# The low halves of the weights in one or in two VectorE instructions: a hybrid encoder with product-key experts, on one core

## The reference, cut to what matters

```
def peer(h, w_query, sub_keys, expert_down, expert_up):
    q = (x @ w_query).reshape(T, PEER_HEADS, 2, D_HALF)
    s = jnp.einsum('thcd,hckd->thck', q, sub_keys).astype(jnp.float32)
    ...
    top_s, pos = lax.top_k(cand, PEER_TOPK)
    idx = jnp.take_along_axis(cidx, pos, axis=-1)
    gate = jax.nn.softmax(top_s, axis=-1).astype(h.dtype)
    ...
        a = jax.nn.gelu(jnp.einsum('cd,chkd->chk', xc, expert_down[ic]))
        return jnp.einsum('chk,chkd->cd', a * gc, expert_up[ic])
```

## Time and profile before

| | us |
|---|---|
| median of three runs | 2186.85 (2167.92 to 2192.66) |
| the profiled execution | 2204.12 |
| its span, first to last instruction | 2202.2 |
| PE busy in it | 1969.0 |
| DVE busy | 1379.8 |
| POOL busy | 666.6 |
| mean granted TensorE clock | 0.933 of full speed |

### The profile page before, as it was taken

How to read it: one execution, slowest core, us unless ns; L and a number is a source line. 1 busy time by engine, 2 the same in 40 slices (tenths; PEclk the granted TensorE clock), 3 DMA queues, 4 the chain that set the end, 5 groups by cost and what they waited for, 6 DMA issues and landing times.

```text
span 2202.2 us, 38709 instructions
## 1 busy us (share of the span) xinstructions
PE 1969.0 (89%) x12144; PEld 1772.9 (81%) x12144; DVE 1379.8 (63%) x2960; ACT 1003.9 (46%) x1638; POOL 666.6 (30%) x627
## 2 busy tenths in 40 slices
PE   7977779668889999999999988797778889999998
PEld 6776779668879888888889987696778788888887
DVE  6855557557535776676567766474556535677666
ACT  5632436245435455444444434353435335544553
POOL 1314538747720000000102023666657710000000
PEclk9988879879989999999999998898889989999999
DMA  6943435334436878888659733353344446787775
GB/s 216 382 159 96 134 114 170 117 107 151 144 127 206 253 243 246 290 287 282 232 168 321 253 134 116 114 173 106 117 127 136 153 134 222 243 241 242 242 241 190
DMA packets 159299, 419.97 MB, mean 191 GB/s; under 512 B 32396, under 2 KB 66220, under 8 KB 158733
## 3 DMA queue, kind: packets, MB, share of 16 engines
q1 hardware_dynamic: 130268, 369.23, 52.5%
q0 software_dynamic: 28976, 50.17, 6.7%
HBM read 382.30 MB, written 37.00 MB: 190 GB/s over the span
## 4 chain that ended last, share of the span: by engine, by line
PE 81%; issue 7%; another core or an unknown queue 5%; ACT 4%; DVE 3%; DMA 1%; POOL 0%; SPq 0%; DVEq 0%; ACTq 0%; POOLq 0%
PE psum L1246 26%; PE psum L1248 26%; PE psum L1247 26%; ACT w_hi L457 1%; DVE w_lo L705 1%; ACT L604 1%; PE psum L1435 1%; ACT L646 1%; PE psum L1412 1%; PE psum L1328 0%; PE psum L1339 0%; ACT big L636 0%; PE psum L1365 0%; DMA raw<-in_attn_units 0%
## 5 line engine op out<-in xcount | busy, mean ns | idle before, releaser
L705 DVE TENSOR_TENSOR w_lo<-raw,w_hi 128x1024 fp32r<-128x1024 f32 x636 | 772.6, 1219 | 455.1 <-ACT w_hi L457 346.0
L1246 PE MATMUL psum<-x_hi,w_hi 128*128 128x256 f32 x2576 | 767.0, 298 | 131.8 <-issue 66.1
L457 ACT CAST w_hi<-raw 128x1024 fp32r<-128x1024 f32 x636 | 663.2, 1048 | 347.1 <-PE psum L1248 330.4
L1247 PE MATMUL psum<-x_lo,w_hi 128*128 128x256 f32 x2576 | 756.7, 294 | 30.0 <-issue 29.5
L1248 PE MATMUL psum<-x_hi,w_lo 128*128 128x256 f32 x2576 | 755.1, 293 | 30.9 <-issue 30.4
L393 POOL DMA_INDIRECT gates<-whole,address x512 | 592.3, 1157 | 408.3 <-issue 159.7
L1246 PEld LDWEIGHTS psum<-x_hi,w_hi 128*128 128x128 f32 x2576 | 519.6, 202 | 160.4 <-issue 101.6
L1248 PEld LDWEIGHTS psum<-x_hi,w_lo 128*128 128x128 f32 x2576 | 519.5, 202 | 35.8 <-issue 35.6
L1247 PEld LDWEIGHTS psum<-x_lo,w_hi 128*128 128x128 f32 x2576 | 520.5, 202 | 33.3 <-issue 32.1
L1246 PE MATMUL psum<-w_hi,l_hi 128*128 128x512 f32 x1152 | 451.5, 392 | 3.4 <-DVE l_lo L1185 2.2
L1248 PE MATMUL psum<-w_hi,l_lo 128*128 128x512 f32 x1152 | 448.5, 389 | 0.0
(11 more groups left out here) (143 smaller groups left out, 1133.6 us busy)
## 6 DMA issues: line engine op xcount, KB each, us to landing
raw<-in_down SPq DMA_DIRECT2D x256, 512.0 KB
raw<-in_up SPq DMA_DIRECT2D x256, 512.0 KB
raw<-in_sg_units SPq DMA_DIRECT2D x72, 512.0 KB
gates<-zeros POOLq DMA_DIRECT2D x64, 512.0 KB, 7.5
g_t<-gates SPq DMA_DIRECT2D x248, 128.0 KB, 4.4
raw<-in_query SPq DMA_DIRECT2D x32, 512.0 KB
raw<-in_attn_units SPq DMA_DIRECT2D x20, 512.0 KB
gates<-whole,address POOLq DMA_INDIRECT x512
```

Source lines behind the costliest of these rows:

```text
L457: act.copy(w_hi[n % SPLIT][:, :], raw[n % RAW][:, :]).then_inc(hi_done, 1)
L705: dve.tensor_tensor(w_lo[n % SPLIT][:, :], raw[n % RAW][:, :], w_hi[n % SPLIT][:, :].bitcast(F32), ALU.subtract).then_inc(lo_done, 1)
L1246: pe.matmul(out_ap, hi_s, hi_m, start=start, stop=False)
L1247: pe.matmul(out_ap, hi_s, lo_m, start=False, stop=False)
```

## The change

In the query and the down stage DVE makes the subtraction of a unit in two instructions of 512 columns, one directly behind the other. The wait for `hi_done` stands ahead of the first, and the increment of `lo_done` is on the second. All other stages keep the single instruction of 1024 columns.

```diff
+            def split_lo_halves(n):
+
+                dve.wait_ge(hi_done, n + 1)
+                for b in range(2):
+                    c = slice(D // 2 * b, D // 2 * b + D // 2)
+                    ins = dve.tensor_tensor(w_lo[n % SPLIT][:, c], raw[n % RAW][:, c], w_hi[n % SPLIT][:, c].bitcast(F32),
+                                            ALU.subtract)
+                ins.then_inc(lo_done, 1)
+
...
                 for c in range(QUERY_UNITS):
-                    split_lo(u["query"] + c + AHEAD)
+                    split_lo_halves(u["query"] + c + AHEAD)
                     dve.wait_ge(s_done, QUERY_UNITS * layer + c + 1)
...
                 def low(n):

-                    split_lo(u["down"] + n + AHEAD)
+                    split_lo_halves(u["down"] + n + AHEAD)
```

## The result

The changed kernel takes 2247.8 us (median of four runs, 2234.83 to 2262.30), the kernel before, run beside it, 2189.76 us (2167.92 to 2213.56). The ratio is 1.030 with a 95% interval of 1.019 to 1.041: slower by 3%, where 2.2% was forecast. The ratio leaves out before's run of 2213.56 us, which counts as a slow one, so it is larger than that of the two medians, which lie 58 us apart. The profiled execution of after took 2244.87 us, 40.8 us more than that of before.

The account below looks back on a forecast made before the run. PE, starved in the query and down stages by the pace of POOL's scatter, bounds the kernel. 45 us lost on PE plus 2 us of DVE on 2204.1 us give 2251, at the median 2235 us; range 2165 to 2305 us.

Parts of the forecast that it names:

- the likeliest case: Whole program: the forecast itself, 2235 us, in a band of 2210 to 2265 us; chance 0.42.
- What bounds the kernel: Query and down stages: PE is starved more the faster POOL issues the scatter; some 295 us lost in the two.
- DVE's own time: Subtraction in query and down: two halves take 0.08 us more, 23 us over 288 units, 2 us counted.
- POOL's locks: Indirect DMAs held by DVE's two-input instructions: halves let POOL in sooner, locks of 101 us fall 21%.
- always-through: POOL always gets through between the halves: locks 52% less, L393's mean 1055 ns, 2299 us; chance above 2265 us 0.14.
- The slope: Query and down: PE loses 2.1 us for each us by which a DMA comes sooner, 45 us in all.
- The signs: Changed profile: L393's mean about 1115 ns, "issue" and eviction waits grow, mean clock below 0.933, up stages and mixers unchanged.
- Never-through: POOL never gets between the halves: locks 9% more, 2170 us; chance 0.23 together with no cause.
- DVE alone: DVE's 23 us are not hidden and POOL changes nothing: 2210 us; chance 0.05.
- Only a companion: The scatter's rate only accompanies PE's stalls: 2170 to 2190 us; chance 0.23 together with never through.
- Faster: POOL never through, longer locks lift windows to a spacing of 1.6 us and more: 2152 us; chance 0.16.
- the prediction's two sentences: Trainium skill: two-input DVE instructions contend with GpSimd reading SBUF; against it, a probe where tensor_tensor did not stall such DMAs.

Follow-up runs that it names:

- the pauses: Three small POOL memsets behind each indirect DMA of the kernel before: 2063.27 us, 0.931 of before's median; with the halves 2046.77 us, 0.924.
- the 64-value DMAs: The kernel before with each indirect DMA writing the values of 64 partitions in place of 128: 2375.99 us, 1.072 of before's median.
- quarters: The subtraction of a query or down unit in four instructions of 256 columns: 2335.03 us, 1.059 of before.

## Why the prediction was right

The time came 13 us above the forecast 2235, inside the 2210 to 2265 of the likeliest case. Step by step:

**What bounds the kernel.** 295 us lost in the two stages were read off the windows; taking the scatter away gave back 292, of which the stages of the profiles account for 272. That the rate is the cause, and not the scatter's presence alone, was argued then and is shown by the pauses (slower pace, 7% faster) and the 64-value DMAs (faster pace, 7% slower).

**DVE's own time.** The forecast was 0.61 us from half to half, 23 us of DVE, 2 us on the path. A half takes 688 ns, the pair 0.07 us more than the single instruction (1.29 us, and not 1.38), DVE is 22 us busier, and without the scatter the halves cost 3.8 us. Right to 2 us. The passage of the Trainium skill that the prediction quoted against its own reading ("VectorE: DVE Perf Modes", section "The DRAIN you can't avoid") adds that an operation that is not held starts earlier, which the prediction left out and the 1.29 us agree with.

**POOL's locks.** The mechanism was as told: a DMA that starts in the first half is done 0.84 us after that half, or after the second. The share was mis-sized. The step "that is undecided, so I take the middle of the ends" gave 21% less and a mean of 1115 ns; the measured 32% and 1094 ns lie nearer to always-through, since 48 of 70 meetings go that way. The count of all 41 meetings, 28 through, would have been the better guide than its 14 with L1024: 68% against the 69% measured.

**The slope.** "2.1 us of PE for each us by which a DMA comes sooner" comes from two of five chosen windows. A line fitted to all 18 runs of at least 14 DMAs without a longer pause in the trace of before has 1.7, one fitted to the 27 of after 1.4. The locks fell by 32 us and the loss through the scatter is 58 - 4 = 54 us by the medians, 1.7 (by the two profiled executions 41 - 4 = 37 us, 1.1). The interval of the ratio, 42 to 90 us in all, leaves 1.2 to 2.7, so 2.1 was probably too steep, but the times alone do not exclude it. Part of the time that POOL gains it spends waiting for gates; that PE recovers there is likely and not shown. The two errors have opposite signs: 32 x 1.7 = 54 us against 21 x 2.1 = 45. A forecast 13 us off was so in part luck. With quarters the loss is steeper again, 116 us for 49 us fewer locks, DVE's own part included, so a fixed slope holds at best near the point at which it was read.

**The signs.** The two stages alone got longer, and the mean clock fell from 0.933 to 0.930, a small step. The eviction wait of PE grew from 43.3 to 55.9 us over the program, as forecast, though it fell in layer 0. "Issue" hardly grew (126.0 to 128.7 us). The name is also less of a cause than the prediction took it for: of the 66.1 us ahead of a unit's first matmul about half, 34.5 us (38.2 of 68.1 in after), is idle time whose weight load starts within 0.06 us of the end of an eviction by ACT, so that part is most likely the eviction wait under another name.

**The rivals.** Never-through falls by the count. DVE alone falls by the run without the scatter. "Only a companion" falls by the pauses. "Faster" was told with a threshold of pace near 1.6 us. On the starving chips slow scatters do lose next to nothing (0.03 us a DMA at 1.68 us in before, 0.05 at 1.88 us with three pauses), and there the halves do win, by the earlier end of the scatter and not by longer locks as this rival had it. The prediction had the loss right for the chip whose profile it read, and no way to see that the chip itself was a condition.

The Trainium skill's "SBUF — State Buffer", section "Who interferes with whom", told of a probe in which tensor_tensor did not stall DMAs that GpSimd issues. By that POOL's mean would have stayed at 1157 ns and the time near 2192. It fell to 1094, and the measurement decides: here a tensor_tensor with two SBUF inputs does stall an indirect DMA, as the first of the prediction's two sentences has it.

**Open:** what PE lacks while the indirect DMAs follow closely; from which pace on, as no run on a starving chip lies between a base of 1.28 and 1.55 us; why the third chip is spared, and whether the chip or the place of the data on it decides; and why the halves in the down stage gain 12 us there, since no trace of before was taken on it. That its scatter ends sooner is likely, as with the pauses, but not shown.

## What to carry to other kernels

A lock between two engines can be what keeps a third one fed: before shortening an instruction that holds up another engine, cut the trace along the work of the one that is held, and see what the others do when it runs free. Small indirect DMAs issued back to back can cost far more than their own time; spacing them out is worth an experiment of four lines, but the pause is paid again where their result is awaited, so it has to end with the slack. And a loss that lives in such contention is measured on more than one chip before a kernel is tuned to it.

## What the runs showed of the hardware

- The same program took 2216 and 2219 us on two chips and 1942 us on a third, with ranges of 4.3, 2.9 and 0.6% of the median. The difference has nearly the size of the scatter's cost.
- 512 indirect DMAs of 128 values each, on a queue of their own and awaited by nobody in these stages, cost 292 us of 2219 on a starving chip, though they move 256 KB in all (512 x 128 x 4 bytes). Half the values in each made it worse (2375.99 us).
- An indirect DMA that starts inside a VectorE instruction with two SBUF inputs, earlier than in its last 0.13 us, ends 0.83 to 0.84 us behind that instruction, or behind the next such one: 1.43 and 1.99 us in after, where an undisturbed one takes 0.96.
- A memset of 2 columns with a wait on the one before, placed behind an indirect DMA, costs 0.02 us: it fits into the 0.30 us that POOL is idle there. Three of them lengthen the period from 1.26 to 1.55 us.
- A DMA of 64 values takes 0.89 us where one of 128 takes 0.96.
